# The low part of each weight chunk, made by GpSimd in two instructions of half the columns with a wait between them

## What is computed

```python
h = rmsnorm(x, norm_g)
proj = h @ w_in                      # queries, keys, values, gates of three kinds of attention
ya, yb, yc = moba(...), dsa(...), dilated(...)
merged = gates_a * (ya @ w_br_a) + gates_b * (yb @ w_br_b) + gates_c * (yc @ w_br_c)
return x + merged @ w_out
```

## Time and profile before

| | |
|---|---|
| median of three runs | 2439.43 us |
| the profiled execution | 2442.71 us, of which span 2440.5 us |
| mean granted TensorE clock | 0.981 |
| TensorE busy | 2326.1 us, 95% |
| GpSimd busy | 1355.8 us, 56% |
| VectorE busy | 1156.3 us, 47% |
| ScalarE busy | 816.6 us, 33% |

### The profile page before, as it was taken

One profiled execution on the slowest core, in us unless ns is written; L12 is line 12 of the kernel. 1 busy time (PEld: TensorE's weight loads), 2 busy tenths in 40 slices (PEclk: granted clock), 3 DMA queues, 4 the chain that ended last, 5 costly groups with the idle time before them and its releaser, 6 DMA issues.

```text
span 2440.5 us, 39512 instructions
## 1 busy us (share of the span) xinstructions
PE 2326.1 (95%) x13560; PEld 2036.2 (83%) x13560; DVE 1156.3 (47%) x2158; ACT 816.6 (33%) x1166; POOL 1355.8 (56%) x714
## 2 busy tenths in 40 slices
PE   7999989899999999999999999999999999778997
PEld 6988989889888888778888888888889789568997
DVE  6653477553765552356655324655325210564233
ACT  4354443544432221303222223222213215214653
POOL 6754778637755554403655543655445447037996
PEclk9999999999999999999999999999999999888999
DMA  7842458524365543302655333655334324014554
GB/s 253 275 131 78 136 197 280 176 81 131 121 216 199 182 146 97 125 9 87 232 182 204 109 95 107 223 189 202 113 91 142 106 96 149 15 35 139 182 171 137
DMA packets 112985, 356.25 MB, mean 146 GB/s; under 512 B 13184, under 2 KB 22912, under 8 KB 112640
## 3 DMA queue, kind: packets, MB, share of 16 engines
q1 hardware_dynamic: 112896, 355.05, 44.9%
HBM read 347.40 MB, written 1.05 MB: 143 GB/s over the span
## 4 chain that ended last, share of the span: by engine, by line
PE 79%; issue 9%; DVE 6%; POOL 4%; ACT 1%; SPq 1%; DMA 1%; DVEq 0%; POOLq 0%; ACTq 0%
PE ps L1768 22%; PE ps L1769 22%; PE ps L1770 22%; POOL w_low L937 3%; PE ps L1876 2%; PE ps L1796 1%; PE ps L1798 1%; PE ps L1797 1%; PE ps L1894 1%; PE ps L1884 1%; PE ps L1927 1%; PE ps L2223 1%; PE ps L2224 1%; PE ps L2225 1%; PE ps L2185 1%
## 5 line engine op out<-in xcount | busy, mean ns | idle before, releaser
L937 POOL TENSOR_TENSOR w_low<-raw,w_high 128x1024 fp32r<-128x1024 f32 (+3 forms) x544 | 1207.0, 2226 | 705.5 <-ACT w_high L539 704.5
L1768 PE MATMUL ps<-h_high,w_high 128*128 128x256 f32 (+1 forms) x2784 | 919.6, 330 | 40.6 <-DVE h_low L1089 18.1
L539 ACT ACTIVATE w_high<-raw 128x1024 fp32r<-128x1024 f32 (+3 forms) x544 | 536.7, 988 | 1205.0 <-PE ps L1770 950.4
L1769 PE MATMUL ps<-h_low,w_high 128*128 128x256 f32 (+1 forms) x2784 | 909.3, 327 | 0.0
L1770 PE MATMUL ps<-h_high,w_low 128*128 128x256 f32 (+1 forms) x2784 | 909.2, 327 | 0.0
L1768 PEld LDWEIGHTS ps<-h_high,w_high 128*128 128x128 f32 x2784 | 535.6, 192 | 90.4 <-issue 23.5
L1769 PEld LDWEIGHTS ps<-h_low,w_high 128*128 128x128 f32 x2784 | 535.7, 192 | 42.6
L1770 PEld LDWEIGHTS ps<-h_high,w_low 128*128 128x128 f32 x2784 | 534.9, 192 | 42.8
L1768 PE MATMUL ps<-act_high,w_high 128*128 128x512 f32 (+1 forms) x770 | 267.7, 348 | 0.0
L1769 PE MATMUL ps<-act_low,w_high 128*128 128x512 f32 (+1 forms) x770 | 267.1, 347 | 0.0
L1770 PE MATMUL ps<-act_high,w_low 128*128 128x512 f32 (+1 forms) x770 | 267.1, 347 | 0.0
(11 more groups left out here) (206 smaller groups left out, 2290.5 us busy)
## 6 DMA issues: line engine op xcount, KB each, us to landing
raw<-in_w_dram SPq DMA_DIRECT2D x216, 512.0 KB, 3.6
raw<-in_wu_dram SPq DMA_DIRECT2D x176, 512.0 KB, 4.5
ada<-in_ada_dram SPq DMA_DIRECT2D x144, 512.0 KB, 4.1
raw<-in_wd_dram SPq DMA_DIRECT2D x64, 384.0 KB, 3.1
raw<-in_wd_dram SPq DMA_DIRECT2D x64, 320.0 KB, 2.9
raw<-in_wv_dram SPq DMA_DIRECT2D x24, 408.0 KB, 4.7
heads<-rot SPq DMA_DIRECT2D x96, 64.0 KB, 3.4
ada<-in_cond_dram SPq DMA_DIRECT2D x6, 512.0 KB, 4.9
```

What stands on the lines that cost most here:

```text
L539: e.activation(wh[:, c % RING, 0:width], raw[:, c % RING, 0:width], ACT.Copy).then_inc(hi_done, 1)
L937: e.tensor_tensor(wl[:, c % RING, 0:width], raw[:, c % RING, 0:width], wh[:, c % RING, 0:width].bitcast(F32), ALU.subtract).then_inc(lo_do ...
L1768: e.matmul(ps[:, bank, to:to + n], wh[:, j, w], hi, start=(first and t == tiles[0]), stop=False)
L1769: e.matmul(ps[:, bank, to:to + n], wh[:, j, w], low, start=False, stop=False)
```

## The change

Instead of one subtraction over all columns of a chunk, POOL issues one over the left half of the columns and one over the right half. Between them it waits for the first half's completion, by a new semaphore, `lo_half`. Only the second half counts `lo_done` up, so all others see the chunk as before.

```diff
         lo_done = sem("lo_done")
+        lo_half = sem("lo_half")
...
             def split(mm, c, width):
                 e.wait_ge(hi_done, mm + 1)
-                e.tensor_tensor(wl[:, c % RING, 0:width], raw[:, c % RING, 0:width],
-                                wh[:, c % RING, 0:width].bitcast(F32), ALU.subtract).then_inc(lo_done, 1)
+                for part in range(2):
+                    here = slice(width // 2 * part, width // 2 * part + width // 2)
+                    if part:
+                        e.wait_ge(lo_half, mm + 1)
+                    e.tensor_tensor(wl[:, c % RING, here], raw[:, c % RING, here],
+                                    wh[:, c % RING, here].bitcast(F32), ALU.subtract)\
+                        .then_inc(lo_done if part else lo_half, 1)
```

## The result

The changed kernel took 2449.07 us (median of 9 runs, 2448.26 to 2452.38) against 2441.32 us for the kernel before in the same comparison (9 runs, 2438.74 to 2444.68): +7.75 us, a ratio of 1.0034 with a 95% interval of 1.0023 to 1.0044. On another chip later, with 11 runs, it was +4.3 us, 1.0018 (1.0009 to 1.0027). It is slower, by 4 to 8 us. The forecast was 2440 us in a range of 2434 to 2449, with 0.80 on "no change that can be told" and 0.14 on slower.

A forecast was written before the change was run, and what follows sets the result against it. TensorE, 79% of the chain, was taken as the bound; POOL's cost counts only where its lead runs out. Terms +5.2 - 4.8 = +0.4 us on the median 2439.4 gave 2439.8, rounded 2440; range 2434 to 2449.

The forecast's parts named there:

- no change that can be told: Whole kernel: result within 7.3 us of no change, the forecast and two of its rivals together; chance 0.80.
- slower: Rival: POOL pays every let-in VectorE instruction in full, in up3, down3 and elsewhere; +15.6 us, 2455; chance 0.14.
- the tail (1 and 2): Last up and down products, up3 and down3: POOL's lead just used up, cost 0, then +3.9 us.
- the starts (3): Five starts at which TensorE waits for a low part: 0.26 us more each, +1.3 us.
- the output product of layer 0 (4): End of out, layer 0: joints let VectorE in earlier, four turns shorter by 0.55 us each, -2.2 us.
- vn to mix (5): Both layers: each joint lets one held VectorE instruction in, the last comes 0.8 us earlier, -1.6 us.
- the branch products (6): br in both layers: with the cast in the joint a turn takes 3.34 us instead of 3.46, -1.0 us.
- up3, cost 0: Last up product: a pair takes 5.95 us against TensorE's 5.76, and POOL's lead of 3.6 us is just used up.
- down3, +3.9: Last down product: no lead left, POOL 0.49 us over TensorE's 7.48 us pace in each of 8 tiles, +3.9 us.
- both rivals on it: up3 and down3: lead holds, down3 costs nothing (2436, chance 0.22); or POOL pays in full, +13.4 us (2455, chance 0.14).
- One sign of the forecast: Profile after, down3: TensorE would wait for low parts by some 4 us in all.
- a rival with 0.06 for the whole: Clock from 343 to 350 us no longer falls, some 3 us back there; whole kernel -8 us, 2431; chance 0.06.

The follow-up runs named there:

- e15: Halves with the wait only in the stages from up0 to ro, against the kernel before: 2445.18 us, +1.2 us, 1.0008.
- e3: Halves everywhere without the wait between them, against the kernel before: 2440.46 us, -3.0 us, 0.9981.
- e7: Halves without the wait only in the mixing, branch and output products of layer 0, against the kernel before: 2440.53 us, -3.6 us, 0.9982.
- e5: Halves with the wait only in the output product of layer 0, against the kernel before: 2440.15 us, -3.9 us, 0.9984.
- e6: Halves with the wait only in the mixing, branch and output products of layer 0, against the kernel before: 2439.50 us, -4.6 us, 0.9983.
- e14: Halves with the wait everywhere except in layer 1, against the kernel before: 2444.60 us, +0.7 us, 1.0006.
- e8: Halves with the wait only in layer 1 (five products), against the kernel before: 2446.50 us, +2.4 us, 1.0010.

## Why the forecast was wrong

The sum had +0.4 us, and at the last chunk the changed kernel is at +6.67. By the table, against the steps: the tail (1 and 2) cost 1.7 us more than forecast, the starts (3) 2.0 more, the output product of layer 0 (4) came out 0.3 better, vn to mix (5) 1.7 worse, and the branch products (6), with the output product of layer 1 behind them, 2.6 worse. Stages that no step has (the first one, rv and ro) gave 1.5 back. So the steps that failed are 5 and 6, and 3 was mis-sized; the tail, the largest term, was nearly right.

1. **up3, cost 0: nearly.** The pair was forecast at 5.95 us and took 5.967. The lead was given out at the end as forecast, and a little before it: +1.1 us.
2. **down3, +3.9: right.** The tile was to take 7.97 us and took 8.03 between the two lines shown; +4.1 to +4.5. The tail as a whole was forecast at 3.9 and measured 5.35, and both rivals on it fell: it neither kept its lead nor paid 13.4. One sign of the forecast did not show: the rows of TensorE's waits have 0.5 us for low parts in down3, and not 4. The loss is seen in the spacing of the tiles and at the last chunk.
3. **The starts, +1.3: mis-sized.** The waits are not for the first chunk of a stage, as the prediction reads them: in up0, up1 and up2 TensorE waits for the fifth chunk, in up2 and rq for the second. Three of the five grew by 0.25 to 0.30 us, as priced. Those in up1 and up2 grew by 0.76 and 0.73: the step left out the instruction that slips into the joint, priced in the tail's step and not here. Two more came that the step did not have: 0.40 us for the fifth chunk of rq, and 0.76 more ahead of up0, where TensorE waits for ScalarE's squares (0.57 before, 1.33 now; 0.57 in e15, with layer 1 whole). The stages behind the starts cost 0.5 to 1.1 us each, 3.3 in the changed kernel's table, 2.1 for the part that e15 has.
4. **Out of layer 0, -2.2: right in mechanism, low in size.** In the changed kernel's table it is -2.5, alone it is -3.9. TensorE's wait fell by 2.6 us (4.4 to 1.77), near the step's 2.2, and part of the clock came back, which the forecast had only as a rival with 0.06 for the whole.
5. **From vn to mix, -1.6: failed by what the step left out.** The stages gained nothing beyond chance, +0.27 and -0.13, though the step's mechanism is there. VectorE's instruction, 2.12 us in the earlier trace rows, takes 0.87 to 1.05 in the joints. The step looked at the joints only and not at when the stretch with them begins. It begins with the high part of mix's first chunk on ACT, behind which the norm's high parts are queued, and that high part waits for its load. The load of that chunk in SP's queue, before and after:

```profile
111.59 1.86 SPq L480 DMA_DIRECT2D heads<-rot  x3
113.84 2.15 SPq L419 DMA_DIRECT2D raw<-in_w_dram  x4
```
```profile
112.63 2.49 SPq L481 DMA_DIRECT2D heads<-rot  x4
115.51 2.15 SPq L420 DMA_DIRECT2D raw<-in_w_dram  x4
```

   The load starts 1.67 us later, 0.55 of which is carried over from the first stage. The high part on ACT starts 1.70 later, and TensorE goes on 0.62 later:

```profile
117.41 1.06 ACT L539 ACTIVATE w_high<-raw 128x1024 fp32r<-128x1024 f32 x1 [2.13 <-DMA raw<-in_w_dram]
...
126.43 2.08 PE L1851 MATMUL ps<-heads 64*128 64x128 f32 x12 [6.32 <-DVE h_low L1261]
```
```profile
119.11 1.06 ACT L540 ACTIVATE w_high<-raw 128x1024 fp32r<-128x1024 f32 x1 [3.28 <-DMA raw<-in_w_dram]
...
127.05 1.23 PE L1857 MATMUL ps<-heads 64*128 64x128 f32 x8 [6.39 <-DVE h_low L1267]
```

   From that high part to TensorE's going on it is 9.02 us before and 7.94 after, and in layer 1 9.04 and 7.97. This holds in every trace: 9.0 to 9.1 us where these low parts are whole, 7.9 to 8.0 where they are halved, with the wait or without (e3). So the joints give 1.1 us, more than the 0.8 forecast, and the late start takes it: counted from the end of vn, the high part comes 1.15 us later in layer 0, where TensorE's wait is as long as before, and 0.5 later in layer 1, where the wait falls from 6.04 to 5.48. That the halves in vn make the load late is argued: SP issues a load only behind its place's low part, those come later in vn, and behind the last of these loads stand the copies for the heads. In the five kernels with halves there the high part of layer 0 starts 1.5 to 2.3 us before the end of vn, against 2.7 before. But it also comes late with nothing halved up to there: in e7 it starts 0.9 us before the end of vn (TensorE's wait is 8.09 us), in layer 1 of e5 0.65 where it was 3.0. What makes it late there is open.
6. **Branch, -1.0 for both layers: half right.** -1.09 in layer 0, more than the step had, and given back one stage on (e6 gains no more than e5 within their intervals), as the waits run together and the clock falls further; +1.47 in br of layer 1, by one longer wait and the clock behind it. The +1.23 in out of layer 1 comes without halves there too (e14). The step had counted turns of POOL and VectorE and nothing of TensorE's waits and its clock. By the medians of e6 and e8, -2.2 us is left of the -4.8 of steps 4 to 6.

Two smaller things. The forecast stood on a median of three runs, 2439.4; nine runs gave 2441.3, so 2 of the 9 us between 2440 and 2449 are in the base. And what 0.3% can tell was taken as 7.3 us for both signs, while the change lies between 4.3 and 7.8, at that edge.

**The cost of POOL in the joint.** Taken as 0.06 to 0.18 us from the row of down3. On the rule that the second engine fully blocks (the Trainium skill, SBUF — State Buffer, "Who interferes with whom") the runs agree for VectorE again: its instructions of 2.35 to 2.56 us beside a whole chunk are 1.51 beside halves and 0.76 to 0.95 beside quarters. POOL did not lose a neighbour's whole length: 0.2 us for a cast of 0.43.

## What to carry to other kernels

Cutting a long instruction of one engine lets the other in earlier, and it does so without a wait in between; the wait costs more than the cut (here 3.7 us against nothing in the tail). Apply such a cut only where the other engine is the one that ends the wait: everywhere and with the wait it cost 4 to 8 us, everywhere without it it gained 3.0, and in one product alone, in quarters without it, 6.4. When an instruction gets shorter, look at what starts the stretch in which it stands: here a load that came 1.1 us later took the 1.1 us that the shorter instructions gave. Before adding small costs up, compare the pace of the engine with the one it feeds and count its lead: two costs that are each free or small can together use the lead up, and from there every tile pays.

## What the runs showed of the hardware

- A wait of POOL for its own instruction costs 0.08 us between two halves of a chunk (78 or 79 ns in all 544), 0.16 ahead of an instruction that itself waits for another engine (the next chunk), and 0.28 ahead of `act_low`.
- The granted clock repaid or doubled small changes of TensorE's waits: the stretch from 343 to 350 us went from 0.56 to 1.00 when 4.4 us of waiting became 1.77, while one wait of 2.36 us instead of 1.07 brought 0.66 from 609 to 614 us in one kernel and none in another.
